# Loading half of the third query chunk earlier, into other buffers, and reordering the slots of the gathered rows

## What is computed

```python
def peer(h, w_query, sub_keys, expert_u, expert_v):
    ...
    def block(xb):
        q = (xb @ w_query).reshape(PEER_BLOCK, PEER_HEADS, 2, PEER_QDIM // 2)
        s = jnp.einsum('thpd,hpnd->thpn', q, sub_keys)
        sv, si = lax.top_k(s, PEER_TOPK)
        ...
        gate = jax.nn.softmax(top_s.astype(jnp.float32), axis=-1)
        act = jax.nn.gelu(jnp.einsum('thkd,td->thk', expert_u[idx], xb).astype(jnp.float32))
        return jnp.einsum('thk,thkd->td', (gate * act).astype(xb.dtype), expert_v[idx])
```

## Time and profile before

| | us |
|---|---|
| median of 3 runs | 1901.68 (1900.18 to 1902.64) |
| the profiled execution | 1899.87 |
| its span | 1898.1 |

### The profile page before, as it was taken

How to read it: one execution, slowest core, us unless ns; L and a number is a source line. 1 busy time by engine, 2 the same in 40 slices (tenths; PEclk the granted TensorE clock), 3 DMA queues, 4 the chain that set the end, 5 groups by cost and what they waited for, 6 DMA issues and landing times.

```text
span 1898.1 us, 13797 instructions
## 1 busy us (share of the span) xinstructions
PE 1595.1 (84%) x4603; PEld 758.1 (40%) x4603; DVE 1086.1 (57%) x1801; ACT 393.9 (21%) x1154; POOL 727.2 (38%) x574
## 2 busy tenths in 40 slices
PE   4999999999999959999977877777777777777776
PEld 1446444556458844443323322222222223222332
DVE  1137896675768784432546646465574655646444
ACT  2001003223011012222212222121231212222112
POOL 0010010001104365555655455554646546555441
PEclk7999999999999989999999999999999999999999
DMA  9999776739987999999999999999999999999997
GB/s 369 387 342 345 285 291 233 271 140 358 371 293 300 412 422 423 422 423 422 423 423 422 422 422 422 422 423 422 422 423 422 422 423 422 423 422 422 423 422 294
DMA packets 147736, 723.63 MB, mean 381 GB/s; under 512 B 10889, under 2 KB 13289, under 8 KB 81106
## 3 DMA queue, kind: packets, MB, share of 16 engines
q0 software_dynamic: 92800, 612.73, 78.6%
q1 hardware_dynamic: 52208, 107.30, 15.4%
q10 hardware_dynamic: 2658, 2.72, 0.6%
HBM read 720.57 MB, written 2.14 MB: 381 GB/s over the span
## 4 chain that ended last, share of the span: by engine, by line
DMA 45%; PE 43%; DVE 5%; POOL 4%; issue 2%; SPq 1%; ACT 1%; DVEq 0%; ACTq 0%
DMA ring<-in_expert_v,acc 17%; DMA H<-in_expert_v,acc 14%; PE ps L995 12%; PE ps L1286 11%; DMA ring<-in_expert_u,acc 7%; PE ps L1130 6%; PE ps L917 3%; PE ps L1245 3%; DMA modrow<-in_expert_v,acc 3%; POOL ring L463 2%; DMA gwork<-in_expert_u,acc 2%; DMA qh<-in_expert_u,acc 2%; PE ps L1186 1%; PE ps L991 1%; PE ps L882 1%
## 5 line engine op out<-in xcount | busy, mean ns | idle before, releaser
L1286 PE MATMUL ps<-ring,wg 128*128 128x512 f32 x1168 | 533.0, 602 | 157.9 <-DMA ring<-in_expert_v,acc 157.9
L1757 DVE SCALAR_TENSOR_TENSOR ring<-ring,A 128x2048 f32<-128x2048 f32 x135 | 308.3, 2291 | 308.2 <-DMA ring<-in_expert_u,acc 308.0
L1286 PEld LDWEIGHTS ps<-ring,wg 128*128 128x128 f32 x1168 | 213.8, 191 | 474.9 <-issue 293.4
L1286 PE MATMUL ps<-H,wg 128*128 128x512 f32 x576 | 263.4, 602 | 64.9 <-DMA H<-in_expert_v,acc 64.9
L463 POOL DMA_INDIRECT ring<-in_expert_v,acc x146 | 199.9, 1369 | 236.3 <-PE ps L1286 225.0
L797 ACT ACTIVATE wg<-K,VX 128x128 f32<-128x128 f32 x256 | 102.8, 402 | 670.8 <-PE ps L1286 669.3
L995 PE MATMUL ps<-ring,H 128*128 128x512 f32 x512 | 222.2, 594 | 1.2 <-ACT VX L594 1.2
L463 POOL DMA_INDIRECT ring<-in_expert_u,acc x135 | 173.4, 1284 | 92.4 <-issue 41.7
L1286 PEld LDWEIGHTS ps<-H,wg 128*128 128x128 f32 x576 | 105.5, 191 | 221.1 <-issue 131.1
L1319 DVE SCALAR_TENSOR_TENSOR acc<-ring,vec,acc 128x512 f32<-128x512 f32 x240 | 180.4, 752 | 21.9 <-DMA ring<-in_w_mod 13.5
L1286 PE MATMUL ps<-modrow,wg 128*128 128x512 f32 x288 | 131.7, 600 | 36.7 <-DMA modrow<-in_expert_v,acc 36.7
(11 more groups left out here) (285 smaller groups left out, 1404.5 us busy)
## 6 DMA issues: line engine op xcount, KB each, us to landing
ring<-in_w_mod POOLq DMA_DIRECT2D x32, 2048.0 KB, 10.4
ring<-in_w_mod SPq DMA_DIRECT2D x32, 1024.0 KB, 14.4
ring<-in_w_in SPq DMA_DIRECT2D x14, 2048.0 KB, 13.2
ring<-in_w_query SPq DMA_DIRECT2D x8, 2048.0 KB, 18.2
ring<-in_w_out SPq DMA_DIRECT2D x12, 1024.0 KB, 12.3
ring<-in_expert_v,acc POOLq DMA_INDIRECT x150, 28.8
ring<-in_expert_u,acc POOLq DMA_INDIRECT x135
B<-in_ctx SPq DMA_DIRECT2D x2, 1024.0 KB, 14.8
```

Source lines behind the costliest of these rows:

```text
L1286: ins = mm(ps[:, 4 * b + n, :], diag[:, r % 4, :], v_rows[r % V_SLOTS][:, n * CH:(n + 1) * CH], start=k == 0, stop=r == BLOCK_RANKS - 1, s ...
L1757: v.scalar_tensor_tensor(out=rows_u, in0=rows_u, scalar=1.0, in1=A[:, r // BLOCK_RANKS, :], op0=ALU.mult, op1=ALU.mult, accum_out=dots[:, ...
```

## The change

Of query chunk 2 the half kh = 1 is no longer loaded into W[3] behind w_free 41. It is loaded as two parts of 1 MB into KT and gwork, behind w_free 38, with a semaphore of its own, ld_wq2; PE reads its weights from there. The slots change: the first ranks use 4, 7, 9, 10, 2, 3 rather than 4, 7, 8, 6, 9, 10, and then 4, 7, 2, 3 in turn; the gather of rank 4 waits for w_free 41. KT and gwork (slots 8 and 6) are first used at ranks 20 and 21. MIDDLE_SLOTS and LATE_SLOTS have a new order.

```diff
-EARLY_SLOTS = (4, 7, 8, 6, 9, 10) + (4, 7, 8, 6) * 3 + (4, 7)
-MIDDLE_SLOTS = (2, 3, 0, 1, 4, 7, 8, 6)
-LATE_SLOTS = (2, 3, 0, 1, 4, 6, 5)
+EARLY_SLOTS = (4, 7, 9, 10, 2, 3) + (4, 7, 2, 3) * 3 + (4, 7)
+MIDDLE_SLOTS = (8, 6, 0, 1, 2, 3, 4, 7)
+LATE_SLOTS = (6, 0, 1, 2, 3, 4, 5)
...
+        fours = lambda row: row.rearrange("p (k n) -> p k n", k=4)
+        WQ2 = {1: [KT[:], fours(gwork[:])], 0: [W[2][:, 0:4], W[2][:, 4:8]]}
...
+            def load_third_query(kh, i, loaded):
+                k0 = (kh * KH + 4 * i) * P
+                sp.dma_start(WQ2[kh][i], w_query[0][k0:k0 + 4 * P, 2 * CH:3 * CH].rearrange(
+                    "(k p) n -> p k n", p=P)).then_inc(loaded, 16)
...
                 load_query(0, kh)
+            sp.wait_ge(S["w_free"], 38)
+            for i in range(2):
+                load_third_query(1, i, S["ld_wq2"])
             for n in range(1, 4):
                 for i, kh in enumerate(HALVES):
+                    if n == 2 and kh == 1:
+                        continue
                     sp.wait_ge(S["w_free"], 36 + 2 * n + i + 1)
                     load_query(n, kh)
...
             for r in range(1, LEAD):
+                if r == EARLY_SLOTS.index(2):
+                    pool.wait_ge(S["w_free"], 41)
                 if r == len(EARLY_SLOTS):
                     pool.wait_ge(S["w_free"], 45)
...
-                    if n == 2:
+                    if n == 2 and kh == 1:
+                        pe.wait_ge(S["ld_wq2"], 32)
+                    elif n == 2:
                         pe.wait_ge(q_ld[kh], 32)
                     else:
                         pe.wait_ge(w_ld[kh], 16 * (8 + n // 2))
-                    wq = W[(2 if n == 2 else 0) + kh]
+                    wq = WQ2[kh] if n == 2 else halves_of(W[kh])
...
-                                     wq[:, k, j * P:(j + 1) * P], h2T[:, kk, :],
+                                     wq[k // 4][:, k % 4, j * P:(j + 1) * P], h2T[:, kk, :],
```

More of the change, by code:

```diff
@@ L257, in build @@
         names = """ym_ready first_picked picked top_ready pick_step ld_id ld_const ld_dft ld_c ld_rows ld_x0 ld_x1 ld_ctx0 ld_ctx1 ld_wg ld_bg ld_gy ld_bm
-        ld_x2 ld_gffn st_mod ld_ga1 ld_sc2 ld_sh2 rows_psum rows_spread ld_keys ld_gfin bg_zero silu_c vec_psum vec_ready vecz_zero vecz_ready moda_free
+        ld_x2 ld_gffn st_mod ld_ga1 ld_sc2 ld_sh2 rows_psum rows_spread ld_keys ld_wq2 ld_gfin bg_zero silu_c vec_psum vec_ready vecz_zero vecz_ready moda_free
         modcol_psum mod_ready ssq std rstd xn_ready xT_psum ht_act ht_dve w_free m_free row_sum
```

## The result

The changed kernel takes 1908.36 us (median of 6 runs, 1907.27 to 1910.51), the kernel before 1901.18 us beside it (1899.09 to 1903.35). The ratio is 1.0038, 95% interval 1.0025 to 1.0051: **slower by some 7.2 us**. The forecast was slower, 1907.0 us, range 1903.0 to 1909.8. The profiled execution's span is 1905.8 us against 1898.1.

A forecast was written before the change was run, and what follows sets the result against it. DMA bytes and idle time were taken to bound the kernel; the early load's 5.0 us gain ended as idle DMA, and rank 39's wait gave a net +5.3 us on 1901.68: 1907.0 us, range 1903.0 to 1909.8.

The forecast's parts named there:

- Bound: From about 590 us the DMA is full at 422 to 423 GB/s; only bytes left and DMA idle time count.
- Part 1: Half of query chunk 2 loaded at about 548 us: costs nothing, removes 5.0 us of DMA after 586.
- Part 2: First ranks in other slots, rank 4 waiting for w_free 41: added wait 0 to 0.3 us, costing nothing.
- Part 3: Rank 22 still waits for w_free 46 at 657.97: DMA runs dry, 1.6 us gained, about 3.4 us idle.
- idle-start row: Profile row of a gather issued to an idle DMA: read 5.85 us after issue; used to price both restarts.
- Part 4: Rank 39 now follows rank 32's dot, issued at about 707.3 with all v gathers behind it: +5.3 us.
- restart: Refilling the empty DMA at rank 39: 5.85 us to its rows, v0 2.48 later; bounds +4.4 to +7.2.
- rank 22's row: Before, rank 22's data was read 7.47 us after issue; taken for the restart's upper bound, +7.2 us.
- (a): Rival: the early load's gain survives, DMA full from 586 to the end, 1896.7 us; chance 0.06.
- the two points: Fixed times the queues cannot last until: 657.97 (rank 22, w_free 46) and 707.04 (rank 32's dot, freeing rank 39).
- (b): Rival: DMA backlog covers the wait at rank 39, leaving 1900.1 to 1901.7 us; chance 0.12.
- (c): Rival: the DMA drains a second time at the v gathers, another restart of about 5 us, 1912; chance 0.05.

The follow-up runs named there:

- e5: Changed kernel with slots reordered so rank 39 follows rank 31 and w_free 46 is waited for at rank 26, not 22: 1896.26 us, ratio 0.9970.
- e8: The changed kernel itself, run again beside a later set: 1909.98 us, ratio 1.0040 to the kernel before.
- e7: Changed kernel with LEAD = 39, so the v gathers are issued ahead of rank 39's gather: 1901.49 us, ratio 0.9999 to the kernel before.
- e1: Changed kernel with another slot order in ranks 28 to 35, so rank 39 follows rank 31, not 32: 1902.27 us, ratio 1.0003 to before.
- e4: Changed kernel in which DVE, after rank 32's dot, waits until rank 39's rows have landed: 1906.52 us, ratio 1.0029 to the kernel before.
- e2: Kernel before with two late slots exchanged, so rank 39 follows rank 32; nothing else of the change: 1908.00 us, ratio 1.0041.
- e3: Changed kernel with the two early query loads put back behind w_free 41, still into KT and gwork: 1908.55 us, ratio 1.0034 to before.

## Why the prediction was right

**Bound.** Right: bytes and idle DMA set the end. The balance (12.9 - 5.0 = 7.9 us) gives the 7.7 us between the two spans within 0.2, and e5 turned 5.0 us of bytes into 5.1 us.

**Part 1, the early load.** Right. The loads were issued at 547 to 548. They landed at 558.4 and 561.1, and nothing waited for them. The remaining half took 16.8 us instead of 44.2.

**Part 2, early ranks.** Right at nothing: from 586 to 646 the DMA moved 404 GB/s, 406 before, and e5, which has these slots too, gained all that the early load saved.

**Part 3, rank 22.** The mechanism was right: the DMA ran dry before w_free 46 (657.38). The size depends on the execution. I had taken the idle-start row, 5.85 us from issue to use, and so 1.6 us of gain. In the profiled one it was 664.52 - 657.38 = 7.14 us, against 7.47 before: 0.3 us. The issue took 2.59 us here, because a dot of DVE had just begun; at the idle-start row it took 1.03, as DVE was picking. In e8 and e7, where POOL was released late in a dot, it took 1.26 and 1.16 us, and issue to use 5.79 and 5.64, near the forecast. From the end of POOL's issue to the use it was 4.5 to 4.6 us in all five traces with the DMA dry here (the changed kernel, e1, e4, e7, e8). So the term left out was the length of the issue. The idle DMA around rank 22 was 0.17 + 1.94 = 2.1 MB or 5.0 us, all that the early load had saved, not 3.4.

**Part 4, rank 39.** Right in the slot, in the releaser and in the time: forecast at 707.3, found at 706.62 in an execution whose stage is 0.6 us early. The term that was mis-sized is the restart: 8.33 us from rank 39's issue to v0's use were taken, with 9.95 as upper bound by rank 22's row, and 10.7 it was, above even that bound (e2, e3 and e8, with the same wait, have 9.9, 9.8 and 11.6). Two things stood in place of the row of the idle start: the issues of rank 39 and v0 took 2.75 and 1.91 us (e4: 0.94 each), and v0's rows came 3.7 us behind rank 39's rather than 2.48 (e4). The sum was +5.3; it became +7.2 by the medians, +7.8 at v0. The median lies inside the range, but it stands where the forecast had its upper bound of +7.2, and e8's median, 1909.98, is just outside the range: that it held owes something to luck. The upper bound came from before's rank 22, whose issue took 1.11 us only the earlier trace rows, so it held nothing of the slow issue either.

**Rivals.** (a) would have been right but for the two points: e5 is that kernel, at 1896.26 us where 1896.7 was the price of (a) (closer than the scatter of the runs allows one to say). (b) fell, since the backlog ended at 703 to 704 (the DMA share is 0.69 in 702 to 704 and 0.03 in 704 to 706). (c) fell: there is no second idle stretch, and behind 720 all is full.

**The estimate by the Trainium skill.** By the Trainium skill's rule for one DMA ("DMA: Bandwidth & Descriptors", Anatomy of one DMA) a gather of this size takes an estimated 4.4 us. e4's first gather, issued in 0.94 us to an idle DMA, took 5.6 us until it was read. The measurement decides: that number would have made the forecast worse. Counted from the end of POOL's issue it was 4.6 us, so most of what is missing in the estimate is the issue itself.

## What to carry to other kernels

Bytes moved into idle time are worth something only if the queue behind them can be filled earlier too: look for the next waits that no data sets (here PE's w_free 46 and DVE's pick), and ask if the queue lasts until then. When slots of a ring are reordered, write out for each rank whose slot it takes over, above all around a long step of the consumer; one rank's distance of 7 in place of 8 cost 7 us, because everything else stood behind it in one engine's order. When an empty queue has to be restarted, price the issues as they are at that moment: rank 39's took 2.75 us in the changed kernel, e2 and e8 and 2.74 in e3, since the dot that frees its slot is followed at once by the next.

## What the runs showed of the hardware

POOL's issue of a gather takes 0.94 us when DVE is still, 0.93 to 1.24 us while it does its small picking operations (the 1.24 is v6's in the earlier trace rows), and 1.1 to 3.0 us when it meets a dot (two inputs of 2048 columns from SBUF), by how much of the dot is left. The issue ends 0.8 us after the end of the dot that ran at its start, in every such issue from 580 to 760 us of the traces of before, the changed kernel, e1 to e5, e7 and e8: in e4 that dot is 712.41 + 2.29 = 714.70 and the issue ends at 713.05 + 2.46 = 715.51; before, rank 22's issue of 657.97 met the last 0.3 us of a dot and took 1.11 us; in the changed kernel it met one that had run for 0.5 us (from 656.87) and took 2.59 us. The issues behind 709.67 follow each other at 2.21 us, as DVE's dots do. The queue being full isn't the cause: at 706.62 it was empty, and e5's v0 was issued in 0.94 us into full queues. The Trainium skill ("SBUF — State Buffer", SBUF: two separate sides) has it that DVE and GpSimd share a pair of ports, which a DVE operation with two SBUF inputs keeps for its whole length against a GpSimd operation that reads SBUF. The rows of e4 agree in kind: issues of 0.94 us before the dots start, 2.46 and 1.91 after; no run here shows the ports themselves.
